# Expert rows added into DRAM by accumulating scatters, and a shorter last stage

## The reference, cut to what matters

```
x = x + mix @ w_o
x = x + hier_moe(rms_norm(x, norm2_g), ...)      # two experts a token
y = rms_norm(x, norm_f_g)

# in hier_moe, for each token t and each of its two choices k:
#   row = (silu(h[t] @ w_gate[e]) * (h[t] @ w_up[e])) @ w_down[e]
#   out[t] += weight[t, k] * row
```

## Time and profile before

| what | us |
|---|---|
| median of three runs | 1763.38 |
| profiled execution, its own time | 1763.4 |
| its span (first to last instruction) | 1761.9 |
| PE busy | 1647.5 (94%) |
| DVE busy | 1029.0 (58%) |
| ACT busy | 835.8 (47%) |
| POOL busy | 140.0 (8%) |
| DMA moved | 304.16 MB, mean 173 GB/s over the span |
| mean granted TensorE clock | 0.970 |

### The profile page before, as it was taken

How to read it: one execution, slowest core, us unless ns; L and a number is a source line. 1 busy time by engine, 2 the same in 40 slices (tenths; PEclk the granted TensorE clock), 3 DMA queues, 4 the chain that set the end, 5 groups by cost and what they waited for, 6 DMA issues and landing times.

```text
span 1761.9 us, 26050 instructions
## 1 busy us (share of the span) xinstructions
PE 1647.5 (94%) x9491; PEld 1471.9 (84%) x9491; DVE 1029.0 (58%) x1780; ACT 835.8 (47%) x1210; POOL 140.0 (8%) x163
## 2 busy tenths in 40 slices
PE   5999999999999999999999998599999999999960
PEld 4899899999998999999999886488888888888850
DVE  5322466665655332114224455688898989888847
ACT  5000355555555331113112222477778787778833
POOL 1100000000000100000000112101111111111000
PEclk9999999999999999999999999699999999999985
DMA  5242111111111311123113522799999999999907
GB/s 160 80 120 84 40 49 37 48 48 36 36 36 47 101 37 48 48 91 101 47 41 123 165 82 102 259 373 386 378 376 374 377 377 384 377 380 373 364 32 288
DMA packets 187892, 304.16 MB, mean 173 GB/s; under 512 B 29364, under 2 KB 91032, under 8 KB 187552
## 3 DMA queue, kind: packets, MB, share of 16 engines
q1 hardware_dynamic: 172688, 267.27, 43.1%
q0 software_dynamic: 15152, 36.18, 5.6%
HBM read 286.97 MB, written 35.19 MB: 183 GB/s over the span
## 4 chain that ended last, share of the span: by engine, by line
PE 92%; DVE 4%; DMA 2%; ACT 1%; issue 1%; POOLq 1%; SPq 0%; POOL 0%; ACTq 0%
PE bank L998 10%; PE bank L669 9%; PE bank L671 9%; PE bank L670 9%; PE bank L986 7%; PE bank L988 7%; PE bank L987 7%; PE bank L814 6%; PE bank L815 5%; PE bank L816 5%; PE bank L763 2%; PE bank L944 2%; PE bank L946 2%; PE bank L948 2%; PE bank L977 2%; PE bank L773 2%
## 5 line engine op out<-in xcount | busy, mean ns | idle before, releaser
L1803 DVE TENSOR_TENSOR e_lo<-e_raw,e_hi 128x2048 fp32r<-128x2048 f32 x192 | 434.2, 2289 | 67.2 <-ACT e_hi L1296 64.7
L1296 ACT ACTIVATE e_hi<-e_raw 128x2048 fp32r<-128x2048 f32 x192 | 366.1, 1926 | 59.3 <-PE bank L988 37.3
L986 PE MATMUL bank<-e_hi,xT_hi 128*128 128x512 f32 x512 | 206.0, 402 | 5.0 <-DVE xT_lo L1808 5.0
L1080 ACT ACTIVATE w_hi<-w_raw 128x1024 fp32r<-128x1024 f32 x68 | 71.7, 1054 | 285.5 <-PE bank L671 252.6
L669 PE MATMUL bank<-h_hi,w_hi 128*128 128x344 f32 x624 | 202.6, 325 | 1.1 <-DVE h_lo L1414 1.1
L988 PE MATMUL bank<-e_hi,xT_lo 128*128 128x512 f32 x512 | 202.9, 396 | 0.0
L987 PE MATMUL bank<-e_lo,xT_hi 128*128 128x512 f32 x512 | 202.6, 396 | 0.0
L670 PE MATMUL bank<-h_lo,w_hi 128*128 128x344 f32 x624 | 199.8, 320 | 0.0
L671 PE MATMUL bank<-h_hi,w_lo 128*128 128x344 f32 x624 | 199.7, 320 | 0.0
L814 PE MATMUL bank<-h_hi,w_hi 128*128 128x344 f32 x576 | 196.6, 341 | 2.0 <-DVE w_lo L1395 2.0
L815 PE MATMUL bank<-h_lo,w_hi 128*128 128x344 f32 x576 | 184.1, 320 | 0.0
(11 more groups left out here) (314 smaller groups left out, 3020.5 us busy)
## 6 DMA issues: line engine op xcount, KB each, us to landing
e_raw<-in_w_e_gate_dram SPq DMA_DIRECT2D x64, 1024.0 KB, 10.2
e_raw<-in_w_e_up_dram SPq DMA_DIRECT2D x64, 1024.0 KB, 11.0
e_raw<-in_w_e_down_dram SPq DMA_DIRECT2D x64, 1024.0 KB, 10.9
w_raw<-in_w_in_dram SPq DMA_DIRECT2D x104, 256.0 KB, 3.2
f_y<-expert_rows SPq DMA_DIRECT2D x16, 512.0 KB, 10.7
a_spill<-y_sb POOLq DMA_DIRECT2D x8, 516.0 KB, 2.9
a_raw<-a_spill SPq DMA_DIRECT2D x2, 2064.0 KB, 9.6
x_tok<-in_x_prompt_dram SPq DMA_DIRECT2D x4, 1024.0 KB, 10.7
```

Source lines behind the costliest of these rows:

```text
L986: pe.matmul(out, xT_hi[:, par, kk, :], wh, start=kk == 0, stop=False)
L1296: A.activation(e_hi[:, slot % 4, :], e_raw[slot][:, :], ACT.Copy).then_inc(e_hi_done, 1)
L1803: V.tensor_tensor(e_lo[slot][:, :], e_raw[slot][:, :], e_hi[:, slot % 4, :].bitcast(F32), ALU.subtract).then_inc(e_lo_done, 1)
```

## The change

There is no `expert_rows` any more. A new DRAM array `summed_rows` (T rows) is first filled by SP with `x2`, tile by tile, in the projection stage (`begin_sums`). ACT multiplies each expert row by its weight on the way from PSUM to `y_out`. For that the weights are needed in the order of the lists: POOL enters them into a second list in DRAM (`weight_lists`) by 18 indirect DMAs behind the first two gathers and reads it back as `wl`. The scatter is now an accumulating one: it adds its rows to `summed_rows` at row `gidx[.., e]`, and each waits for the one before. In the last stage SP loads 9 tiles in place of 18, straight into `f_out`; `combine` is gone; the load of `n_ov` by POOL stands ahead of the last two scatters; the drain is a plain semaphore increment; and ACT issues one small square root beforehand (`warm`).

```diff
+            def begin_sums(n, rows):
+                sp.wait_ge(x2_done, n + 1)
+                sp.dma_start(sum_dram[bass.ds(n * P, rows), :], x2[0:rows, bass.ds(n, 1), :]...).then_inc(sums_begun, 16)
...
             with sp.Fori(1, 4) as i:
                 for b in range(2):
                     load_x(i * 2 + b, b, False)
+                    begin_sums(i * 2 + (b - 2), P)
             sp.wait_ge(sq2_done, 7)
             sp.dma_start(x_in[0:B8, 0, :], x_sample[:, 0, :]).then_inc(x_again[0], 16)
+            begin_sums(6, P)
             sp.wait_ge(proj_done, NT)
             for s in range(4, 12):
                 if s == 9:
+                    begin_sums(7, P)
+                    begin_sums(8, B8)
                     for par in range(2):
                         sp.wait_ge(gathered[par], 16)
                 load_chunk(s, (s - 4) % 6, 1 + (s - 4) // 6, None)
...
             for n in range(NT):
                 rows = P if n < 8 else B8
-                for k in range(2):
-                    sp.dma_start(f_y[k][0:rows, n, :], y_dram[n * P + k * T:n * P + k * T + rows, :]).then_inc(f_loaded[n], 16)
+                sp.dma_start(f_out[0:rows, n, :], sum_dram[n * P:n * P + rows, :]).then_inc(f_loaded[n], 16)
...
             pool.dma_start(list_dram.rearrange("(p q) o -> p (q o)", p=P), list_init[:, :]).then_inc(list_blank, 16)
+            pool.dma_start(wl_dram.rearrange("(p q) o -> p (q o)", p=P), list_init[:, :].bitcast(F32)).then_inc(list_blank, 16)
...
             def scatter_rows(e):
                 pool.wait_ge(y_stored, e + 1)
-                pool.indirect_dma_start(out=y_dram, out_offset=bass.IndirectOffsetOnAxis(ap=lst[:, e:e + 1], axis=0),
-                                        in_=y_out[:, :], in_offset=None, bounds_check=2 * T - 1, oob_is_err=False).then_inc(scattered, 16)
+                if e > 0:
+                    pool.wait_ge(scattered, 16 * e)
+                pool.indirect_dma_start(out=sum_dram, out_offset=bass.IndirectOffsetOnAxis(ap=gidx[:, e:e + 1], axis=0),
+                                        in_=y_out[:, :], in_offset=None, bounds_check=T - 1, oob_is_err=False,
+                                        compute_op=ALU.add).then_inc(scattered, 16)
+
+            def enter_weights(n, rows):
+                for k in range(2):
+                    pool.indirect_dma_start(out=wl_dram, out_offset=bass.IndirectOffsetOnAxis(ap=adr[0:rows, 2 * n + k:2 * n + k + 1], axis=0),
+                                            in_=wts[0:rows, n, k:k + 1], in_offset=None, ...).then_inc(weighed, 16)
 
             for e in range(2):
                 gather_rows(e)
+            pool.wait_ge(wts_done, 1)
+            for n in range(NT):
+                enter_weights(n, P if n < 8 else B8)
             for e in range(NE):
                 if e + 2 < NE:
                     pool.wait_ge(xT_psum, e + 1)
                     gather_rows(e + 2)
+                if e == 0:
+                    pool.wait_ge(weighed, WEIGHED_FROM + 32 * NT)
+                    pool.dma_start(wl[:, :], wl_dram[0:P * NE, :].rearrange("(r e) o -> r (e o)", e=NE)).then_inc(wl_loaded, 16)
+                    pool.wait_ge(sums_begun, SUMS_FROM + 16 * NT)
                 if e >= 2:
                     scatter_rows(e - 2)
+            pool.wait_ge(ov_sbuf, 3)
+            n_ov = pool.value_load(ov_t[0:1, 2 * OVF:2 * OVF + 1], min_val=0, max_val=OVF)
             for e in range(NE - 2, NE):
                 scatter_rows(e)
             pool.wait_ge(scattered, 16 * NE)
-            pool.wait_ge(ov_sbuf, 3)
             pool.sem_inc(v_free, 1)
-            n_ov = pool.value_load(ov_t[0:1, 2 * OVF:2 * OVF + 1], min_val=0, max_val=OVF)
...
-            pool.drain().then_inc(rows_written, 1)
+            pool.sem_inc(rows_written, 1)
...
                 if not first:
                     act.wait_ge(scattered, e * 16)
+                else:
+                    act.wait_ge(wl_loaded, WL_FROM + 16)
                 for x in range(2):
-                    ins = A.activation(y_out[:, 512 * x:512 * x + 512], bank[2 + x][:, :], ACT.Copy)
+                    ins = A.activation(y_out[:, 512 * x:512 * x + 512], bank[2 + x][:, :], ACT.Copy, scale=wl[:, e:e + 1] if isinstance(e, int) else wl[:, bass.ds(e, 1)])
...
-            act.wait_ge(rows_written, 1)
+            A.activation(warm[:, :], eps[:, :], ACT.Sqrt)
             for n in range(NT):
                 rows = P if n < 8 else B8
-                act.wait_ge(f_sum, n + 1)
+                act.wait_ge(f_loaded[n], F_FROM + 16)
...
-            step.after(V.tensor_tensor(wts[:, :, 1], wts[:, :, 1], wts[:, :, 0], ALU.mult))
+            V.tensor_tensor(wts[:, :, 1], wts[:, :, 1], wts[:, :, 0], ALU.mult).then_inc(wts_done, 1)
...
-            for n in range(NT + 1):
-                if n < NT:
-                    combine(n)
-                if n > 0:
-                    finish(n - 1)
+            for n in range(NT):
+                finish(n)
```

More of the change, by code:

```diff
@@ L111, in program @@
     xn_dram = nc.dram_tensor("normed_rows", (T, D), F32).ap()
-    y_dram = nc.dram_tensor("expert_rows", (2 * T, D), F32).ap()
+    sum_dram = nc.dram_tensor("summed_rows", (T, D), F32).ap()
+    wl_dram = nc.dram_tensor("weight_lists", (LISTROWS * NE, 1), F32).ap()
     list_dram = nc.dram_tensor("token_lists", (LISTROWS * NE, 1), U32).ap()
@@ L261, in program @@
         scol = small("scol", [1], U32)
+        wl = small("wl", [NE])
+        wcol = small("wcol", [1])
+        warm = small("warm", [1])
         e_raw = [at(f"e_raw{i}", RING + 8192 * i if i < 4 else 8192 * (i - 4), [2048]) for i in range(12)]
@@ L279, in program @@
         v_aT = at("v_aT", R3 + 4096, [4, P])
-        f_y = [at(f"f_y{k}", 36864 * k, [NT, D]) for k in range(2)]
         f_out = at("f_out", R5, [NT, D])
@@ L340, in program @@
             sem("v_gu"), sem("v_silu"), sem("v_act"), sem("v_apsum"), sem("v_aT_done"), sem("v_ypsum"), sem("v_y"), sem("v_scattered"))
-        rows_written, gf_loaded, f_sum, f_sq, f_root, f_done, f_stored = (
-            sem("rows_written"), sem("gf_loaded"), sem("f_sum"), sem("f_sq"), sem("f_root"), sem("f_done"),
-            sem("f_stored"))
+        rows_written, gf_loaded, f_sq, f_root, f_done, f_stored = (
+            sem("rows_written"), sem("gf_loaded"), sem("f_sq"), sem("f_root"), sem("f_done"), sem("f_stored"))
+        wts_done = sem("wts_done")
+        sums_begun, SUMS_FROM = x_loaded[0], 16
+        weighed, WEIGHED_FROM = cols_loaded, 32
+        wl_loaded, WL_FROM = consts_loaded, 16 * 4
         f_loaded, F_FROM = e_loaded[0:NT], 16 * 16
@@ L449, in load_chunk @@
                              w[bass.ds(ex, 1), :, ks, :].rearrange("e p k f -> p (e k) f")).then_inc(e_loaded[slot], 16)
+            def begin_sums(n, rows):
+                sp.wait_ge(x2_done, n + 1)
+                sp.dma_start(sum_dram[bass.ds(n * P, rows), :], x2[0:rows, bass.ds(n, 1), :].rearrange("p a d -> p (a d)")).then_inc(sums_begun, 16)
             load_x(0, 0, True)
@@ L575, in _ @@
             pool.dma_start(rb[:, NG:NG + NE], b_router_expert[0].partition_broadcast(P)).then_inc(router_loaded, 16)
-            pool.wait_ge(list_blank, 16)
+            pool.wait_ge(list_blank, 32)
             def write_xn(n, rows):
@@ L619, in scatter_rows @@
                 pool.wait_ge(y_stored, e + 1)
-                pool.indirect_dma_start(out=y_dram, out_offset=bass.IndirectOffsetOnAxis(ap=lst[:, e:e + 1], axis=0),
-                                        in_=y_out[:, :], in_offset=None, bounds_check=2 * T - 1, oob_is_err=False).then_inc(scattered, 16)
+                if e > 0:
[6 more added lines that the diff above has]
+                    pool.indirect_dma_start(out=wl_dram, out_offset=bass.IndirectOffsetOnAxis(ap=adr[0:rows, 2 * n + k:2 * n + k + 1], axis=0),
+                                            in_=wts[0:rows, n, k:k + 1], in_offset=None,
+                                            bounds_check=LISTROWS * NE - 1, oob_is_err=False).then_inc(weighed, 16)
             for e in range(2):
                 gather_rows(e)
+            pool.wait_ge(wts_done, 1)
+            for n in range(NT):
+                enter_weights(n, P if n < 8 else B8)
             for e in range(NE):
@@ L644, in _ @@
                         pool.dma_start(scol[:, 0:1], list_dram[bass.ds(bk * (P * NE), P * NE), :].rearrange("(r e) o -> r (e o)", e=NE)[:, bass.ds(ex, 1)],
+                                       allow_slow_non_contiguous=True).then_inc(v_col, 16)
+                        pool.dma_start(wcol[:, 0:1], wl_dram[bass.ds(bk * (P * NE), P * NE), :].rearrange("(r e) o -> r (e o)", e=NE)[:, bass.ds(ex, 1)],
                                        allow_slow_non_contiguous=True).then_inc(v_col, 16)
@@ L652, in _ @@
                         carry(1).then_inc(idled, 1)
-                        pool.indirect_dma_start(out=y_dram, out_offset=bass.IndirectOffsetOnAxis(ap=scol[:, 0:1], axis=0),
```

(13 more changed lines are left out.)

## The result

The changed kernel takes 1780.69 us in the median of four runs (1777.72 to 1783.12), the kernel before 1763.63 (1762.5 to 1764.55). The ratio is 1.0096, 95% interval 1.0079 to 1.0114: 17 us slower, where 17 us faster was forecast. The profiled execution took 1777.72 with a span of 1776.2, 14.3 us over that of before.

A forecast was written before the change was run, and what follows sets the result against it. PE was taken to bound the expert loop, with the DMA engines full but hidden, and DMA the last stage. 1763.4 - 27.7 + 0.5 + 10.3 = 1746.5 us; range of 8 in 10: 1734 to 1785.

The forecast's parts named there:

- Part 1, the last stage: After the last copy to `y_out`: 27.7 us saved, 8.2 by an earlier start of SP's loads, 19.5 after it.
- the last scatter: Last stage: the accumulating scatter lands in 4.2 us, range 3.2 to 7.3, where a plain one took 3.18.
- Part 2, gather 2: Before the loop: 18 weight entries take 23.2 us, gather 2 lands 5 us early; no cost, upper end 5 us once.
- Part 3, the loop: Accumulating scatters in the expert loop: reading old rows loads the DMA engines until PE waits for weights, 10.3 us in all.
- X: Added engine time per expert in the loop for reading old rows: 0.69 us taken, from 0 to 2.07.
- 0.69 us each: Loop: q0's 22 gathers and 22 scatters took 30.4 us of all 16 engines, 0.69 us each.
- the prediction's own formula: Loop cost: 28.2 experts x (0.245 us backlog each + X) - 16.1 us of room, not below 0.
- The dear rows: Rival, chance 0.28: adding rows cost several plain ones; loop loses 29.7 us (1766) at X = 1.38, 49.2 (1785) at 2.07.
- The room of 23.9 us: Loop: a weight chunk is issued 8 chunks before its split, so landing up to 23.9 us stays hidden.
- X = 1.29: Loop: the value where 28.2 x 1.535 equals 16.1 + 27.2; dearer rows would make the kernel slower.
- The rival of a free read: Loop: DMA has room, X stays below 0.33 and is covered, 1736 us; chance 0.19.
- that of the drain: Last stage: the drain did not take the 8.4 us, SP starts as before, less 1; 1754 to 1755 us; chance 0.10.

The follow-up runs named there:

- e6: The kernel before with POOL's drain alone replaced by a plain semaphore increment: 1756.58 us against 1764.98 for the kernel before, run beside it.
- e1_spread: The changed kernel with both lists read back dealt out over all partitions, in four reads each: 1748.04 us, ratio to before 0.9915.
- e7_upper_half: The changed kernel with both lists read back so that entries 0 to 63 stand on partitions 64 to 127: 1781.27 us, ratio 1.0087.
- e2: The changed kernel with the accumulate taken out of the loop's scatters, so rows overwrite and the sum is not made: 1742.24 us, ratio 0.9876.
- e5: The changed kernel with the token list spread over partitions and weights gathered from a table by token, without the 18 entries: 1739.14 us, ratio 0.9856.
- e3: The kernel before with only the token list spread over the partitions: 1765.73 us, ratio 1.0008.

## Why the prediction was wrong

**Part 1, the last stage: right.** Of 27.7 us 25.2 came. The 8.4 us were the drain's own (e6). From SP's first load to the end it took 24.7 us (1751.52 to 1776.2), predicted 24.2. The term that was most off is the last scatter: 5.78 us against 4.2. It too depends on the spread: 4.34 in e1_spread, 5.84 in e7_upper_half, 3.18 for a plain one in e2.

**Part 2, gather 2: the upper end was too low.** I took 1.29 us an entry from a pair of the stage before. Here 18 took 33.2 us (1116.20 to 1149.43), 1.85 each, just over the 1.8 that I had named as the end; gather 2 landed at 1157.5, 5.7 after PE wanted it. The rest of the 8.4 is TensorE's clock: idle for these 6 us, it made the transposes in 1.97 us (0.88 before) and its next down product in 7.17 (5.46 before), with a granted clock of 0.63 of full speed where the kernel before has 1.00 from 1157 to 1165 us. The stretch, columns as in the earlier trace rows:

```profile
1157.00:1165.00 8.00, 7.46 (x26) 6.29 (x27) 1.29 (x2) 2.09 (x3) 1.00 (x1) 0.63 0.51 165
```

POOL's and DVE's timeline shows why an entry takes long, and the group row of the entries their spread (ns):

```profile
1132.38 2.29 DVE L1839 TENSOR_TENSOR e_lo<-e_raw,e_hi 128x2048 fp32r<-128x2048 f32 x1 [0.93 <-ACT e_hi L1329]
```

```profile
1132.60 2.92 POOL L644 DMA_INDIRECT weight_lists<-wts,adr  x1 [0.30 <-issue]
1135.82 0.97 POOL L644 DMA_INDIRECT weight_lists<-wts,adr  x1 [0.30 <-issue]
```

```profile
L644 POOL DMA_INDIRECT weight_lists<-wts,adr x18: 872/1444/2917, 1116.2 to 1148.3; - x18
```

The entry shown first begins while DVE makes a low part and ends 0.85 us after that instruction (1134.67, then 1135.52). So do all nine that begin so, 0.77 to 0.90 us after it; the other nine take 0.87 to 1.00, two of them begun while DVE made `xT_lo`, whose one input lies in PSUM. It was to be had before: one gather of the kernel before, at 1243.7 us, met the same instruction and took 3.2 us, where the median was 1.02. No run here took DVE's work away, so this is read from the trace, not tested. The Trainium skill (SBUF — State Buffer, section "Who interferes with whom") says that a DVE instruction with two inputs in SBUF contends with a GpSimd instruction that reads SBUF; the trace agrees.

**Part 3, the loop: this step failed, and it turned the sign.** The mechanism was the predicted one (second reads, growing landing, splits that wait), and even the price of a row: q0's 11.0% of 400 us is 44.0 us for 21 pairs, 2.10 a pair, less 0.69 for the gather 1.41; X = 0.71, predicted 0.69. The failing sentence is "0.69 us each", of all 16 engines, and the X taken from it: a cost spread evenly over the 16. With every row on half of them it is twice that on each, 1.42, and the prediction's own formula gives 28.2 x (0.245 + 1.42) - 16.1 = 30.9 us; measured 31.1. So near a match is in part luck: with the 1.75 that the row counts give it would be 28.2 x (0.245 + 1.24) - 16.1 = 25.8, and where the other 5 us come from stays open. The pace points the same way. From 1178 to 1357.5 us the transposes of successive experts lie 17.9 us apart, and from there for 18 experts 19.63 in the mean, which is 1.70 more, where the two forms of the formula have 1.67 and 1.49.

The dear rows were priced at 29.7 with X = 1.38, so the rival named the right size for the wrong reason. What I had in hand against the sum: 64 rows of 128 partitions, and the rule of the Trainium skill cited under theory A. The loop alone turned the sign: with 31.1 in place of 10.3 the sum is 1767.3. Gather 2 (7.9 more than forecast) and the last stage (2.5 less saved) bring it to the 1777.7 of the profiled execution. The room of 23.9 us is not contradicted, since no split waited in e5 with landings up to 18.2 us; X = 1.29 as the point from which it decides was not tested.

The rival of a free read is out by e2 against the changed kernel, that of the drain by e6. That the engines "are full" in the kernel before was not true of all: spread (e3), they moved the same bytes with a flat landing.

## What to carry to other kernels

A mean share over 16 DMA engines hides an uneven load: before adding work to a queue ask on which partitions its rows lie, and deal short lists out over all of them (a list of up to 64 of 128 entries left half of the engines out); here this was worth 33 us for a few small reads. A landing time that crept up under a busy PE was here a sign of overloaded engines behind a mean that looked like a limit; what is added there is paid once the prefetch room is gone. A run of small GpSimd DMAs is priced beside the DVE work that it will meet, not by the quiet stage where the row was read.

## What was not expected of the hardware

- A row of 4 KB added into DRAM takes its engine twice the time of a written one (packets of 327 ns against 159; 1.41 us against 0.69 for some 64 rows, as a mean over 16 engines).
- POOL's drain behind indirect DMAs, all of them landed, took 8.4 us where an increment took 0.03.
- SP's DMAs of 4-byte elements held SP for 10 us in all in e5_spread_table, for four issues; the longest, 5.8 us, was that of a DMA of 8 elements behind one of 1024.
